# Attention softmax: the second head's probabilities are scaled by ScalarE instead of VectorE

## The reference, cut to what matters

```python
s = jnp.einsum('bqhgd,bkhd->bhgqk', qi, k_all)   # kind A; 128 queries at a time
p = softmax_f32(s, v_all.dtype)                  # exp(s - max) / sum
return jnp.einsum('bhgqk,bkhd->bqhgd', p, v_all)
...
p = softmax_f32(jnp.concatenate([s_nb, s_ctx], axis=-1), v.dtype)         # kind B
...
p = softmax_f32(jnp.concatenate([s, s_ctx, s_sink], axis=-1), v.dtype)    # kind C
```

## Time and profile before

| | |
|---|---|
| median of 3 runs | 2999.24 us (2999.14 to 3002.69) |
| profiled execution, its own time | 3004.67 us |
| its span in the trace | 3002.9 us |
| mean granted TensorE clock | 0.98 |
| PE busy | 2843.1 us, 95% |
| DVE busy | 1351.1 us, 45% |
| ACT busy | 748.0 us, 25% |
| POOL busy | 177.8 us, 6% |

### The profile page before, as it was taken

How to read it: one execution, slowest core, us unless ns; L and a number is a source line. 1 busy time by engine, 2 the same in 40 slices (tenths; PEclk the granted TensorE clock), 3 DMA queues, 4 the chain that set the end, 5 groups by cost and what they waited for, 6 DMA issues and landing times.

```text
span 3002.9 us, 33599 instructions
## 1 busy us (share of the span) xinstructions
PE 2843.1 (95%) x13144; PEld 1506.8 (50%) x13144; DVE 1351.1 (45%) x2564; ACT 748.0 (25%) x1355; POOL 177.8 (6%) x225
## 2 busy tenths in 40 slices
PE   7998999999999899999999999999999998999998
PEld 3555555665555556566544544444443434444442
DVE  2796776775356564574475841111113523111112
ACT  3233354441222354332261120000002122000001
POOL 1323212100011100000000000000000000000000
PEclk9999999999999999999999999999999999999999
DMA  7344223111144432102111048999993216999996
GB/s 287 110 143 144 95 85 98 51 71 56 56 155 164 150 113 99 43 29 112 47 56 42 28 182 339 421 421 421 421 421 156 80 74 273 409 421 421 422 420 276
DMA packets 90670, 586.56 MB, mean 195 GB/s; under 512 B 10192, under 2 KB 10192, under 8 KB 29232
## 3 DMA queue, kind: packets, MB, share of 16 engines
q1 hardware_dynamic: 69696, 502.56, 41.6%
q0 software_dynamic: 20848, 82.26, 8.5%
HBM read 582.68 MB, written 2.10 MB: 195 GB/s over the span
## 4 chain that ended last, share of the span: by engine, by line
PE 68%; DVE 6%; ACT 2%; DMA 1%; issue 1%; DVEq 0%; ACTq 0%
PE BIG L1022 44%; PE PJ L1022 10%; PE BIG L1812 4%; PE PT L1347 2%; PE PT L1364 2%; PE PT L1022 1%; DMA W<-in_mod_rows 1%; PE BIG L1325 1%; PE PJ L1071 1%; PE BIG L1329 1%; PE PT L1788 1%; ACT ARENA L2012 0%; DVE SPILL L2310 0%; DVE ARENA L2853 0%; PE BIG L1318 0%
## 5 line engine op out<-in xcount | busy, mean ns | idle before, releaser
L1022 PE MATMUL BIG<-ARENA 128*64 128x512 f32 (+3 forms) x2608 | 542.0, 463 | 4.8 <-DVE ARENA L2875 2.5
L1022 PE MATMUL PJ<-HT,W 128*128 128x512 f32 (+2 forms) x1040 | 396.8, 531 | 13.9 <-DVE ARENA L2408 5.5
L1022 PEld LDWEIGHTS BIG<-ARENA 128*64 128x64 f32 (+1 forms) x2608 | 283.2, 168 | 249.9 <-issue 221.7
L1022 PE MATMUL BIG<-HT,W 128*128 128x512 f32 (+1 forms) x768 | 320.2, 578 | 2.4 <-DVE ARENA L2710 2.1
L1022 PE MATMUL BIG<-W,ARENA 128*64 128x512 f32 (+1 forms) x1280 | 282.3, 573 | 0.9 <-DVE ARENA L2756 0.9
L1022 PEld LDWEIGHTS PJ<-HT,W 128*128 128x128 f32 x1040 | 193.3, 192 | 174.1 <-issue 134.2
L2904 DVE SCALAR_TENSOR_TENSOR XC<-BIG,MOD,XC 128x512 f32<-128x512 f32 x128 | 90.2, 746 | 381.1 <-PE BIG L1812 381.1
L2023 ACT ACTIVATE ARENA<-PT 128x512 f32<-128x512 f32 (+1 forms) x264 | 144.5, 583 | 457.8 <-PE PT L1347 457.5
L2310 DVE CUSTOM_DVE_ANT_0 SPILL<-W,VEC 128x1024 bf16<-128x1024 f32 x168 | 223.1, 1328 | 56.1 <-DMA W<-in_mod_rows 48.4
L1022 PEld LDWEIGHTS BIG<-HT,W 128*128 128x128 f32 x768 | 146.5, 191 | 173.0 <-issue 165.9
L1022 PEld LDWEIGHTS BIG<-W,ARENA 128*64 128x64 f32 (+1 forms) x1280 | 112.2, 142 | 156.5 <-issue 143.5
(11 more groups left out here) (301 smaller groups left out, 2897.2 us busy)
## 6 DMA issues: line engine op xcount, KB each, us to landing
ARENA<-in_exp_w SPq DMA_DIRECT2D x168, 1024.0 KB, 18.1
W<-in_exp_w SPq DMA_DIRECT2D x144, 1024.0 KB, 16.7
W<-in_units SPq DMA_DIRECT2D x89, 1024.0 KB, 4.9
HT<-in_exp_w SPq DMA_DIRECT2D x72, 1024.0 KB, 21.8
W<-in_mod_rows POOLq DMA_DIRECT2D x128, 512.0 KB, 3.9
ARENA<-in_bias_b POOLq DMA_DIRECT2D x16, 384.0 KB, 4.2
XC<-in_x SPq DMA_DIRECT2D x1, 3072.0 KB, 10.5
XC<-in_x POOLq DMA_DIRECT2D x1, 3072.0 KB, 12.0
```

The source lines that it names most:

```text
L1022: ins = pe.matmul(out, lhsT, rhs, start=start, stop=stop, skip_group_check=skip)
```

## The change

The second head's probabilities are no longer scaled by VectorE. VectorE still takes both inverses. Having taken the second, it signals `second_sum` and goes on. ScalarE, after its two exponentials of a step, waits for that signal and multiplies the second head's probabilities in place with a copy whose scale is the column of inverses, and signals `second_scaled`, for which TensorE waits before it transposes the second head. In all 120 steps one VectorE multiplication goes and one ScalarE instruction comes.

```diff
@@ TensorE, T @@
                             if y == 0:
-                                pe.wait_ge(probs_scaled, me.next("probs_scaled"))
+                                if h == 0:
+                                    pe.wait_ge(probs_scaled, me.next("probs_scaled"))
+                                else:
+                                    pe.wait_ge(second_scaled, me.next("second_scaled"))
@@ ScalarE, E @@
                             act.activation(PROB[:, h, 0:b - a], BIG[h][:, a:b], ACT.Exp, bias=STAT[:, c:c + 1],
                                            accum_out=STAT[:, 4 + c:5 + c]).then_inc(probs_exp, 1)
+                        act.wait_ge(second_sum, me.next("second_sum"))
+                        probs = PROB[:, 1, 0:min(b, NA) - a]
+                        act.activation(probs, probs, ACT.Copy, scale=STAT[:, 8 + c:9 + c]).then_inc(second_scaled, 1)
@@ VectorE, E @@
                             dve.wait_ge(probs_exp, me.next("probs_exp"))
-                            link(dve.reciprocal(STAT[:, 8 + c:9 + c], STAT[:, 4 + c:5 + c]))
+                            inverse = dve.reciprocal(STAT[:, 8 + c:9 + c], STAT[:, 4 + c:5 + c])
+                            if h == 1:
+                                inverse.then_inc(second_sum, 1)
+                                continue
+                            link(inverse)
```

More of the change, by code:

```diff
@@ L639, in build @@
         probs_scaled = sem("probs_scaled")
+        second_sum = sem("second_sum")
+        second_scaled = sem("second_scaled")
         t_filled = sem("t_filled")
```

## The result

The changed kernel takes 3044.42 us, the median of 4 runs (3040.34 to 3048.73), against 3000.97 for the kernel before on the same chip (4 runs, 2999.14 to 3003.19). The ratio is 1.014, 95% interval 1.0125 to 1.0156: slower by 1.4%. The prediction was 3043, in a range of 3015 to 3062, with a chance of 0.87 for slower. The profiled execution of the changed kernel took 3043.35 us, with a span of 3041.5, 38.6 more than before.

The account below looks back on a forecast made before the run. TensorE was taken to bound the kernel. Stalls of 21 + 8.4 + 0.4 + 4.2 + 7.6 less 5.2 gained gave 36.4, plus 7 for clock: about +44 us, so 2999.24 becomes 3043, range 3015 to 3062.

Parts of the forecast that it names:

- The wait is what costs: ScalarE's queue waits for VectorE's second inverse, so product readings come late (up to some 3.3 us) and TensorE stalls.
- What it named as signs: VectorE some 65 us less busy, ScalarE 80 more; first-layer TensorE waits for ScalarE's readings 25 us or more; clock lower.
- What it removes and adds: All 120 steps: some 65 us of VectorE multiplications go; ScalarE instructions like 690 and 900 ns exponentials come.
- First layer, B: Late readings at 24 steps of the first layer's B pairs: stalls of 29 us, net 21 after absorption.
- First layer, A and C: Late readings in the first layer's other pairs: 8.4 us in A after 0.6 absorbed, 0.4 in C.
- Second layer, B: 3.2 us at three pairs' last tile absorbed by load waits; fourth pair 3.3 + 0.95: 4.2 us.
- Second layer, A and C: Later copies of transposes, 2.1 us, and six later rope ends, 5.5 us: sum 7.6.
- The clock: About eight added TensorE waits over 2 us, half dropping the granted clock: 7 us, bounds 0 and 13.
- Gains: VectorE freed just ahead of things TensorE waits for, at a few places in both layers: 5.2 us.
- Sum: Whole kernel: stalls less gains 36.4 us, plus 7 for the clock, about +44 us.
- That most would be absorbed: Rival: later waits in the same step, or an earlier inverse, absorb most stalls; 3006 to 3025 us, chance 0.20.
- The faster one: Rival: VectorE's relief and less contention with GpSimd shrink TensorE's waits; 2988 to 2993 us, chance 0.07.

Follow-up runs that it names:

- e3: Kernel before, VectorE still multiplying both heads, with only ScalarE's wait for the second inverse added: 3032.04 us, ratio 1.0097.
- e1: Changed kernel with ScalarE's wait and multiplication moved behind the readings of products, at the step's output item: 3000.60 us, ratio 0.9991 to the kernel before.
- e11: Changed kernel with ScalarE's wait and multiplication moved behind the readings of products in the first layer only: 3019.77 us, ratio 1.0052 to the kernel before.
- e7: Changed kernel with ScalarE multiplying after its reading for rope at the last tile of the second layer's A and C pairs: 3031.01 us, ratio 1.0091.
- e2: Changed kernel with ScalarE's copy at scale 1.0, waiting only for its own exponential, second head left unnormalised: 3004.30 us, ratio 1.0003 to the kernel before.
- after again: The changed kernel, unaltered, measured and profiled a second time: 3044.15 us (2 runs).

## Why the prediction was right, and where it was off

The mechanism was the one forecast, and it is shown: the wait alone costs 29 us (e3), the work and signal behind the readings cost nothing on balance (e1), and moving wait and work together removes all of the first layer's loss (e11) and 13.0 of the second's 19.6 us with eight steps (e7). "The wait is what costs" holds for the first layer; in the second the copy itself, ahead of the readings, costs more than the wait (e2, e3). The prediction's moved readings contain both, so its sum isn't touched by that.

What it named as signs came. TensorE's waits for ScalarE's readings of products grew from 6.4 to 40.9 us over the span (three groups), where it had called those of before near nothing. By its steps:

- **What it removes and adds.** VectorE's -65 us came out at -60.8, ScalarE's +80 at +85.5. The instruction that the trace of before didn't have takes, in the groups by shape,

```profile
L2021 ACT ACTIVATE ARENA<-ARENA,STAT 128x512 f32<-128x512 f32 x48 | 34.7, 723 | 81.2 <-DVE STAT L2461 81.2
...
L2021 ACT ACTIVATE ARENA<-ARENA,STAT 128x768 f32<-128x768 f32 x32 | 30.0, 937 | 20.5 <-DVE STAT L2461 20.5
```

  723 and 937 ns, against the exponential's 690 and 900 taken for it: 0.03 to 0.04 us more each, below 1 us over the places that count. A nearer row than the exponential was in the trace of before: ScalarE's in-place pass over 128x512 with a column as bias (L1899), 720 ns. The idle times say more: 1.7 us (81.2 / 48) ahead of one of 512 columns, 0.6 ahead of one of 768, in pairs where fewer modulation items stand in the way (48 in the 40 steps of the A pairs, 119 in the 40 of the B pairs).
- **First layer, B.** The gross stalls were nearly right in sum: 29 forecast. In the waits of TensorE from 89.7 to 360 us of the changed kernel stand

```profile
PE PJ L1024 <- ACT ARENA L1967: 21.2, 13, 3.6
PE PJ L1262 <- ACT ARENA L1967: 6.8, 2, 4.4
```

  28.0 us, and 2.9 in the same pairs before, so 25 new. What was off more is how much other waits give back. Those others fell from 24.3 to 9.5 us, by 14.8, where the prediction had 8 absorbed and 1.85 gained. So the waits grew by 10.3, against 21.3 - 1.85 = 19.4 forecast. The time of the four pairs grew by 15.0 (255.3 to 270.3), nearer to the forecast by what it had not in this term: 1.2 of clock, and what many short waits cost beyond their length (below). The stretches of each layer's pairs, B, A and C, of the kernel before:

```profile
90.20:345.50 255.30, 228.22 (x1153) 138.50 (x1152) 201.39 (x401) 85.43 (x197) 73.33 (x82) 0.97 0.43 138
345.50:547.30 201.80, 190.40 (x1143) 116.90 (x1142) 140.31 (x270) 95.03 (x194) 37.22 (x43) 0.99 0.27 87
...
836.10:1054.80 218.70, 199.37 (x1003) 121.91 (x1002) 128.18 (x253) 58.40 (x129) 26.53 (x50) 0.96 0.47 156
1054.80:1224.00 169.20, 157.10 (x971) 95.42 (x970) 94.80 (x177) 73.55 (x138) 11.00 (x19) 0.99 0.29 100
1224.00:1328.80 104.80, 99.67 (x652) 60.27 (x651) 71.07 (x193) 46.06 (x105) 0.00 (x0) 1.00 0.12 41
```

  and of the changed one:

```profile
89.70:360.00 270.30, 232.37 (x1153) 138.60 (x1152) 189.67 (x376) 98.64 (x220) 73.12 (x82) 0.97 0.40 130
360.00:567.40 207.40, 191.80 (x1143) 117.41 (x1142) 126.30 (x246) 113.23 (x219) 38.24 (x43) 0.98 0.26 84
...
856.20:1080.10 223.90, 202.47 (x1003) 124.54 (x1002) 120.42 (x237) 69.75 (x144) 26.53 (x50) 0.95 0.46 152
1080.10:1258.00 177.90, 160.39 (x971) 97.13 (x970) 86.10 (x161) 88.57 (x154) 10.72 (x19) 0.97 0.28 95
1258.00:1368.50 110.50, 102.87 (x652) 62.52 (x651) 63.60 (x178) 57.33 (x120) 0.00 (x0) 0.97 0.11 39
```

- **First layer, A and C.** The second row: 207.4 from 201.8, 5.6 more, 8.4 - 2.7 = 5.7 forecast. So close an agreement is partly luck: the waits over 0.25 us grew by 3.5, and 1.1 is clock. C took 0.4 more (134.0 to 134.4), 0.4 forecast.
- **Second layer, B.** The third row: 223.9 from 218.7, 5.2 more, 4.2 forecast. Here too the number is better than the reason: the waits grew by 2.1 us and 3.5 is clock, which this term did not have.
- **Second layer, A and C.** The last two rows: 8.7 and 5.7, 14.4 more together, against 7.0 forecast without the clock. The waits are as forecast, 7.8 more (17.1 to 24.9 us); the rest is the clock, whose busy time at half speed went from 3.4 to 16.8 us in these pairs, 6.7 lost. The clock is the term that was mis-sized. The prediction had counted about eight waits of over 2 us, most of them in the first layer, and 7 us for them in the total, within bounds of 0 and 13. It was 12.5 (10.2 and 2.3), and four fifths of it fell in the second layer. There waits that had been up to 1.8 us grew to 2.7, and the half clock doubled. The prediction looked for waits that were long; it should have looked for those that an added microsecond makes long.
- **Gains.** At 172.04 TensorE waited 2.02 us. After the change, at the same place:

```profile
177.60 1.29 DVE L2467 TENSOR_SCALAR ARENA<-ARENA,STAT 128x512 f32<-128x512 f32 x1
...
179.63 0.88 PE L1024 MATMUL PJ<-HT,W 128*128 128x384 f32 x2 [0.84 <-DVE ARENA L2416]
```

  1.18 less, 1.05 forecast. The multiplication that stayed is as slow beside GpSimd's sums as both were. The whole group of such readings fell from 7.7 to 4.9 us.
- **Sum.** By layer the forecast without the clock was 25 and 11 us, and 7 for the clock, 43 in all. The traces have 18.7 and 9.4 without the clock, and 12.5 for it, 41 in all. So 6 too much in the first layer and 2 in the second stood against 5 too little for the clock. That the median came within 2 us of 3043 is partly luck.
- **Rivals.** That most would be absorbed (chance 0.20) had a true core: other waits gave back 14.8 us in the first layer's B pairs, gains included. The faster one (0.07) was wrong for this placement, but its gain exists: the first layer of e2, where the wait is gone, ran 7.0 us below the kernel before.

The 5.0 us of the first layer that waits over 0.25 us and the clock leave are mostly waits as well. Two things are missing from the 13.7: the shorter waits (all waits together grew by 15.0, 43.1 to 58.1), and a loss at each. Where TensorE had not to wait, the profile shows a group of 128x384 matmuls to begin 0.16 us before the one ahead has ended (before, at 91.70: 1.78 us long, and the next at 93.32); behind a wait it begins after that end. There are 55 waits instead of 42, so about 2.1 us more by this estimate. With 2.3 of clock that is 19.4 of the 21.0.

Left open are the last 1.6 us, and what decides whether the clock falls behind a given wait.

## What to carry to other kernels

A wait put into an engine's in-order queue is paid for by whatever stands behind it. Before moving work to an engine with idle time, look up in the timeline when its input is ready and what the next instruction there sets free; if the input is late, queue the work behind that instruction. Here the place of wait and work was 43 us; behind the readings the work cost nearly nothing, ahead of them it cost 12.7 us in the second layer even without the wait. And go through the waits that TensorE has already and that the change makes longer, not only the new ones: in the A and C pairs of the second layer 7.8 us more of them cost 14.4 us, because the granted clock fell behind some.

## What the runs showed of the hardware

- The granted clock reacts to which waits there are, and traces repeat it: 41.0, 37.5 and 41.0 us at half clock in the second layer of three kernels with the same second layer (after, after again, e11), 20.5 and 23.9 in two traces of the one before. In the first layer the same program gave 23.9, 30.7 and 34.1. Seven executions of e11 fell into two groups, 3013.5 to 3014.5 us at 0.984 to 0.985 and 3019.8 to 3025.0 at 0.981 to 0.982.
- Half clock costs time as far as TensorE is busy in it. Counted so, waits and clock give 20.0 us for the second layer of the change (19.6 measured) and 13.1 for e7 (13.0 measured). Before the change TensorE was idle for 6.1 of the second layer's 20.5 us.
- No length of a single wait decides over the clock. The changed kernel shows 2.70 us followed by 0.50 at 1119.40 and 2.70 us followed by 1.00 at 1197.10; e7 shows 1.97 us followed by 0.50 and 1.54 followed by 1.00; before, 2.56 was followed by 1.00.
- ScalarE's in-place copy is a little dearer with a column as scale: 0.72 us for 512 columns and 0.94 for 768 here, against 0.63 and 0.85 with a constant of 1 (e2).
